# Second head pair's key squares ahead of the first columns, an early one-column exponential, and V's ones and a weight split behind two exponentials

## The chip, the cores and the metric

The kernel runs on one core of one Trainium2 chip. The metric is the device time of one execution in microseconds; the kernel before has a median of 856.37 us over three runs (855.74 to 856.46). The core's engines run apart from one another and meet only at semaphores: TensorE (PE: matmuls and transposes), VectorE (DVE), ScalarE (ACT), GpSimd (POOL) and the DMA queues, most of whose transfers SyncE (SP) issues. Each engine takes its instructions strictly in the order in which the program lists them, so an instruction that waits also holds everything queued behind it on its engine.

## The reference

One layer of a streaming encoder, for 512 prompt tokens and 32 sample tokens, all in float32, shortened:

```python
xn = rms_norm(x, g_mix_norm)
c_q, c_kv, k_r, u, gate_a, gate_b = split(xn @ w_in)
q = rms_norm(c_q, g_q_a) @ w_q_b                 # 16 heads of 64 + 32
kv = concat(past_lat, rms_norm(c_kv)) @ w_kv_b   # keys 64, values 64 per head
s = rms_norm(q_nope) . rms_norm(k_nope) + rope(q_rope) . rope(k_r)
attn = softmax(mask(s * scale)) @ v              # chunk-causal, 16 heads
u_c = causal_dwconv(u, width 4)                  # 1024 channels
r, i = sigmoid(u_c @ w_rg), sigmoid(u_c @ w_ig)
a = exp(-8 r softplus(-lam)); h_t = a h_(t-1) + sqrt(1 - a^2) i u_c
x = x + (sigmoid(gate_a) attn + sigmoid(gate_b) h) @ w_out
up = causal_dwconv(rms_norm(x, g_ffn_norm) @ w_up, width 3)
x = x + (silu(gate) * val) @ w_down
```

The layer is computed for the prompt (no past) and for the sample (512 cached positions).

## The kernel before

**Numbers as two halves.** Every large product is made in three passes. A weight tile of 128 columns (an "item", 128x1024) comes by DMA into `w_raw`; ScalarE rounds it into `w_hi` (`split_hi`), VectorE subtracts to get the rest, `w_lo` (`split_lo`), and TensorE multiplies hi·hi, hi·lo and lo·hi. Items 4 to 15 are the columns of `w_in` that stand ahead of attention; items 16 onward (`I_IN + 12` is item 16) are gate columns, multiplied inside the attention. SyncE issues the load of item t only when `w_lo` of item t-4 is done.

**Stages.** Up to 80 us the latents and the first columns are made. Then eight channel blocks of the gated recurrence run beside the first products: each block needs a convolution, two sigmoids, a tanh, an exponential, a square, a square root and a scan along time on VectorE (`recurrence(n)`, which raises the semaphore `recurrence_done`). At about 146 us the attention starts: eight steps `attend(p)`, each for one pair of heads, until about 405 us. After it come the output product and the feed-forward block, in which TensorE multiplies almost without a break.

**The order is written out by hand.** Each engine has its own block with its own `attend(p)`, and its place in the list decides when something is done; nothing is reordered by a scheduler. A step p has nine score tiles, n = 0 to 8. For a tile TensorE multiplies queries and keys (`scores`), VectorE takes the row maximum (`row_max`), ScalarE the exponential (`exps`), TensorE transposes the probabilities (`transpose_probs`), ScalarE copies them to SBUF (`probs_columns`), and TensorE multiplies them with V (`values`). `scores(p, n)` for n from 2 on waits for the exponential of tile n-2.

**The preparation of the pairs is laced into it.** For pair q ScalarE copies key and query products out of PSUM (`evacuate_kq`), squares the keys (`squares_keys`, into the buffer `kqs`) and then the queries (`squares_queries`, into the same buffer, so after VectorE's `key_sums`); VectorE sums the squares (`key_sums`, `query_sums`), takes inverse roots by ten small chained steps (`inverse_roots`) and scales keys and queries; GpSimd rotates the queries. While `attend(0)` runs for pair 0, pair 1 is normalised and pair 2 is projected. In VectorE's `attend(0)` the order is row maximum of tile 2, query sums of pair 1, inverse roots, row maximum of tile 3.

**Two guards at the entry.** The first `probs_columns` waits for more than its transpose, because its target shares memory with a recurrence buffer:

```python
act.wait_ge(s_pt, p * 9 + (n + 1))
...
if p == 0 and n == 0:
    act.wait_ge(s_rec, 6)
```

`s_rec` is `recurrence_done`, and the sixth scan is `recurrence(5)`. And `values(0, 0)` waits for `value_ones(0)`, three ScalarE copies that write the ones beside V from which the softmax sums come. ScalarE's functions come in tables; the exponential needs another one than the square root, and a load stands in the program (ACT_TABLE_LOAD) where it changes. Copy and Square need no load.

Of the kernel before, what the change touches and what calls it, by code (L numbers as in the profile page):

```python
# [20 lines left out]
P = 128  # L21
# [115 lines left out]
def layer(nc, i, c, o):  # L137
# [3 lines left out]
    with ctx:  # L141
# [9 lines left out]
        def fixed(name, shape, dtype=F32):  # L151
            nonlocal place
            n = int(np.prod(shape[1:])) * 4
            t = at(name, shape, place, dtype)
            place += -(-n // 32) * 32
            return t
# [13 lines left out]
        raw = fixed("w_raw", [P, 4, KD * P])  # L170
        hi = fixed("w_hi", [P, 2, KD * P], F32R)
        lo = fixed("w_lo", [P, 2, KD * P], F32R)
        region = place

        U = fixed("U", [P, KD, LEAD + TU])
# [506 lines left out]
        def _(act):  # L682
# [151 lines left out]
            def split_item(t):  # L834

                split_hi(t, t, loaded(t))
# [15 lines left out]
            def squares_keys(q):  # L852

                kn3 = Kn[q % 2][:, :, :, :].rearrange("p t h n -> p (t h n)")
                act.wait_ge(s_kqf, q * 6 + 3)
                if q == 0:
                    act.wait_ge(s_rec, 3)
                else:
                    act.wait_ge(s_kqm, q * 2)
                    act.wait_ge(s_qr, q)  # L860
                nc.scalar.activation(kqs[:, :], kn3, ACT.Square).then_inc(s_kqs, 1)
# [17 lines left out]
            def value_ones(s):  # L879

                if s == 0:
                    act.wait_ge(s_iu, KD - 1)
                    act.wait_ge(s_lru, KD)
                else:
                    act.wait_ge(s_rec, KD)
                full = NKT - 1
                nc.scalar.activation(V[:, s, 0:full, 1, :], ones[:, 0:VD].unsqueeze(1).to_broadcast([P, full, VD]), ACT.Copy)
                nc.scalar.activation(V[LASTP:, s, full, 1, :], ones[LASTP:, 0:VD], ACT.Copy)
                nc.scalar.activation(V[0:LASTP, s, full, :, :].rearrange("p h n -> p (h n)"), zero[0:LASTP, 0:1].to_broadcast([LASTP, 3 * VD]),
                                     ACT.Copy).then_inc(s_clear, 1)  # L890
# [14 lines left out]
            def probs_columns(p, n):  # L905

                act.wait_ge(s_pt, p * 9 + (n + 1))
                if p or n >= 2:
                    act.wait_ge(s_pv, p * 9 + n - 1)
                if p == 0 and n == 0:  # L910
                    act.wait_ge(s_rec, 6)
                b = (n + p) % 2
                w = width(n) if n < 8 else 2 * P + R2
                nc.scalar.activation(PT[:, b, 0:w], PS[:, 6 + b, 0:w], ACT.Copy).then_inc(s_ptf, 1)  # L914
# [21 lines left out]
            def columns_left(q, v, bank):  # L936

                par, bank = q % 2, PS[:, bank, :]
                act.wait_ge(s_tr, q * 5 + (v + 1))
                if q == 1 and v == 0:  # L940
                    act.wait_ge(s_bt, 6)
                if v < 2:
                    last = nc.scalar.activation(KT[0:NOPE, 2 * par + 1, v * 512:(v + 1) * 512], bank[NOPE:, :], ACT.Copy,
                                                scale=gkn[NOPE:, :])
                else:
                    if q == 0:
                        act.wait_ge(s_m2, KD)
                    last = nc.scalar.activation(QT[0:QK, 2 * par, 0:SEQ], bank[0:QK, :], ACT.Copy)
                last.then_inc(s_tra, 1)

            def attend(p):

                kq, following = p + 2 < NP_, p + 1 < NP_
                for n in range(9):
                    if n < 8:
                        exps(p, n + 1)
                    elif following:
                        exps(p + 1, 0)
                    probs_columns(p, n)
                    if kq and n < 3:  # L960
                        evacuate_kq(p + 2, 2 * n, 0)
                        evacuate_kq(p + 2, 2 * n + 1, 1)
                    if n == 0 and p == 0:
                        squares_queries(1)
                        act.wait_ge(s_free, 11)
                        gate_tanh(gate("A", 1))
                    if n == 1 and p == 0:
                        split_item(I_IN + 13)
                        act.wait_ge(s_free, 12)
                        gate_tanh(gate("B", 1))  # L970
                    if n == 1 and 1 <= p <= 5:
                        act.wait_ge(s_gf, 4 * p)
                        gate_tanh(gate(*gate_of(15 + 2 * p)))
                        split_item(17 + 2 * p)
                    if following and n == 3:
                        columns_left(p + 1, 0, 0)
                        columns_left(p + 1, 1, 1)
                    if following and n == 5:
                        columns_left(p + 1, 3, 1)
                    if n == 5 and p < 7:  # L980
                        split_item(18 + 2 * p if p < 5 else 23 + p)
                    if p == 7 and n == 6:
                        output_split_hi(2)
                    if n == 4 and kq:
                        squares_keys(p + 2)
                    if p == 0 and n == 6:
                        last_states()
                    if n == 7:
                        head_sums(p, 0)
                        if kq:  # L990
                            squares_queries(p + 2)
                    if n == 6:
                        if p == 0:
                            value_ones(1)
                        if following:
                            evacuate_v(p + 1, 0, 1)
                            act.wait_ge(s_gf, 2 * (fills(p)[0] - I_G) + 2)
                            gate_tanh(gate(*gate_of(fills(p)[0])))
                    if p == 6 and n >= 6:
                        mixed_hi(n - 6)  # L1000
                    if p == 7 and n < 3:
                        mixed_hi(3 + n)
                    if p == 7 and n == 8:
                        mixed_hi(6)
                if following:
                    evacuate_v(p + 1, 1, 0)
                    evacuate_v(p + 1, 2, 1)
                head_sums(p, 1)
                sample_parts(p)
# [30 lines left out]
                evacuate_kq(1, u, 4 + u)  # L1040
            for u in range(4, 6):
                evacuate_kq(1, u, u - 4)
            split_item(I_IN + 12)
            for v in (0, 1, 3):
                columns_left(0, v, 4 + v)
            for u in range(3):
                evacuate_v(0, u, (0, 1, 7)[u])
            exps(0, 0)
            value_ones(0)
            squares_keys(1)  # L1050
            for p in range(NP_):
                attend(p)
            output_split_hi(3)
# [65 lines left out]
        def _(dve):  # L1119
# [120 lines left out]
            def recurrence(n):  # L1240

                a_n = U[:, n, LEAD:]
                dve.wait_ge(s_h0, n + 1)
                nc.vector.tensor_tensor_scan(a_n, a_n, uc(n), 0.0, ALU.mult, ALU.add).then_inc(s_rec, 1)
# [33 lines left out]
            def key_sums(q):  # L1278
                dve.wait_ge(s_kqs, q * 2 + 1)
                nc.vector.tensor_reduce(small[:, 0, 0:NKH], sq3, X, ALU.add).then_inc(s_kqm, 1)  # L1280
# [40 lines left out]
            def row_max(p, n):  # L1321

                dve.wait_ge(s_s, p * 9 + (n + 1))
                bank, sm = score_bank(p, n), small[:, 4 + n % 3, :]
                if n < 8:
                    nc.vector.tensor_reduce(sm[:, 2:3], bank[:, 0:width(n)], X, ALU.max, negate=True).then_inc(s_mx, 1)
                else:
                    link(nc.vector.tensor_reduce(sm[:, 3:4], bank[:, 0:HP], X, ALU.max, negate=True))
                    nc.vector.tensor_reduce(sm[0:R2, 4:5], bank[0:R2, HP:HP + DEC], X, ALU.max, negate=True)
                    link(nc.vector.tensor_copy(sm[0:R2, 5:6], sm[R2:, 3:4]))  # L1330
                    link(tt(sm[0:R2, 2:3], sm[0:R2, 3:4], sm[0:R2, 4:5], ALU.min))
                    link(tt(sm[0:R2, 2:3], sm[0:R2, 2:3], sm[0:R2, 5:6], ALU.min))
                    nc.vector.tensor_copy(sm[R2:, 2:3], sm[0:R2, 2:3]).then_inc(s_mx, 1)

            def split_item(t):

                split_lo(t, t)
# [198 lines left out]
            columns(0, 4, 3)  # L1536
            row_max(0, 0)
            row_max(0, 1)
            recurrence(5)
            split_item(I_IN + 12)  # L1540
            key_sums(1)
            for p in range(NP_):
                attend(p)
            gated_sample(7)
# [645 lines left out]
```

## Time and profile before

| | us |
|---|---|
| median of three runs | 856.37 |
| the profiled execution, its own time | 856.38 |
| its span in the trace | 854.6 |
| PE busy | 837.5 (98%) |
| DVE busy | 569.0 (67%) |
| ACT busy | 363.2 (43%) |
| POOL busy | 201.0 (24%) |

The profile page gives each engine's busy time in the span, the chain of waits that ended last, and groups of instructions. Below it, the timeline lists single instructions of one engine: when they start and how long they take, where a start may come before the end of the one ahead (the engine overlaps them), so that the step from start to start is what an instruction costs its queue. An idle time stands in brackets, with what ended it.

### The profile page before, as it was taken

What the parts mean: (1) busy time and instruction counts of PE and PEld (TensorE: products, weight loads), DVE (VectorE), ACT (ScalarE), POOL (GpSimd) and SP (SyncE); (2) the same over time, 40 slices, a digit from 0 to 9 for tenths busy, and PEclk for the clock granted to TensorE, in tenths of its full rate; (3) what the DMA queues carried; (4) which work ended last, traced back from release to release, by engine and by line L of the source; (5) the groups of instructions that cost most, each with busy time, mean ns of one, the idle gap of its engine ahead of it and who ended that gap; (6) DMA issues with size and microseconds to landing.
All of it is one profiled execution on the core that took longest, in us unless ns stands there. A gap on an engine that the chain in (4) does not pass through costs nothing.

```text
span 854.6 us, 16810 instructions
## 1 busy us (share of the span) xinstructions
PE 837.5 (98%) x6540; PEld 801.0 (94%) x6540; DVE 569.0 (67%) x1059; ACT 363.2 (43%) x606; POOL 201.0 (24%) x229
## 2 busy tenths in 40 slices
PE   7999999999999999999999999999999999999998
PEld 6999898889998899877999999999999999999998
DVE  5695779877667676787646888888777776222121
ACT  5636859666545565566245222222212221222121
POOL 3122213202112021121140444333443344010000
PEclk9999999999999999999999999999999999999999
DMA  8533321131110200100222233232332323233321
GB/s 227 143 91 87 101 54 35 41 81 39 41 50 17 53 26 29 50 5 23 74 87 87 74 99 98 74 98 77 94 90 82 93 73 94 86 106 100 106 57 41
DMA packets 114467, 63.73 MB, mean 75 GB/s; under 512 B 7660, under 2 KB 112878, under 8 KB 114412
## 3 DMA queue, kind: packets, MB, share of 16 engines
q1 hardware_dynamic: 112428, 59.25, 24.5%
q0 software_dynamic: 1936, 3.70, 1.8%
q8 instruction: 38, 0.62, 0.3%
q14 instruction: 17, 0.14, 0.1%
q10 hardware_dynamic: 48, 0.02, 0.0%
HBM read 59.85 MB, written 2.70 MB: 73 GB/s over the span
## 4 chain that ended last, share of the span: by engine, by line
PE 86%; DVE 7%; ACT 4%; issue 2%; DMA 0%; SPq 0%; POOL 0%; ACTq 0%; POOLq 0%; DVEq 0%
PE PS L1650 47%; PE PS L1819 9%; PE PS L1902 6%; PE PS L1874 4%; PE PS L1836 4%; PE PS L1778 2%; PE PS L1856 2%; PE PS L2109 2%; PE PS L1810 2%; PE PS L1708 2%; PE PS L1774 1%; PE PS L1741 1%; PE PS L1800 1%; DVE w_lo L1129 1%; PE PS L1662 1%
## 5 line engine op out<-in xcount | busy, mean ns | idle before, releaser
L693 ACT ACTIVATE w_hi<-w_raw 128x1024 fp32r<-128x1024 f32 (+2 forms) x102 | 105.5, 1034 | 291.4 <-PE PS L1650 280.8
L1129 DVE TENSOR_TENSOR w_lo<-w_raw,w_hi 128x1024 fp32r<-128x1024 f32 (+2 forms) x102 | 126.0, 1235 | 106.2 <-ACT w_hi L693 106.1
L1650 PE MATMUL PS<-x2h,w_hi 128*128 128x272 f32 x704 | 145.7, 288 | 0.0
L1650 PE MATMUL PS<-x2h,w_lo 128*128 128x272 f32 x704 | 145.7, 288 | 0.0
L1650 PE MATMUL PS<-x2l,w_hi 128*128 128x272 f32 x704 | 145.1, 288 | 0.0
L1650 PEld LDWEIGHTS PS<-x2h,w_hi 128*128 128x128 f32 x704 | 110.8, 188 | 0.1
L1650 PEld LDWEIGHTS PS<-x2l,w_hi 128*128 128x128 f32 x704 | 110.6, 189 | 0.0
L1650 PEld LDWEIGHTS PS<-x2h,w_lo 128*128 128x128 f32 x704 | 109.9, 189 | 0.0
L654 POOL TENSOR_TENSOR uct<-uct 128x512 f32<-128x512 f32 x22 | 28.4, 1293 | 165.0 <-DVE uct L1603 165.0
L1650 PE MATMUL PS<-hh,w_hi 128*128 128x272 f32 x308 | 64.2, 289 | 0.0
L1650 PE MATMUL PS<-hh,w_lo 128*128 128x272 f32 x308 | 63.8, 289 | 0.0
L1650 PE MATMUL PS<-hl,w_hi 128*128 128x272 f32 x308 | 63.5, 288 | 0.0
L1819 PE MATMUL PS<-xnh,w_hi 128*128 128x272 f32 x192 | 57.2, 298 | 0.2 <-DVE KT L1313 0.2
L1819 PE MATMUL PS<-xnh,w_lo 128*128 128x272 f32 x192 | 55.6, 290 | 0.0
L1819 PE MATMUL PS<-xnl,w_hi 128*128 128x272 f32 x192 | 55.1, 287 | 0.0
L585 POOL TENSOR_TENSOR rot<-Qn,rope 128x320 f32<-128x320 f32 x16 | 14.5, 924 | 169.8 <-DVE Qn L1303 169.8
L914 ACT ACTIVATE PT<-PS 128x128 f32<-128x128 f32 (+4 forms) x72 | 31.3, 434 | 52.0 <-PE PS L1856 48.6
L1836 PE MATMUL PS<-KT,QT 100*128 100x128 f32 (+3 forms) x128 | 46.8, 448 | 3.6 <-ACT Pn L900 2.4
L1650 PEld LDWEIGHTS PS<-hh,w_hi 128*128 128x128 f32 x308 | 48.4, 188 | 0.1
L1650 PEld LDWEIGHTS PS<-hl,w_hi 128*128 128x128 f32 x308 | 48.4, 188 | 0.0
L1650 PEld LDWEIGHTS PS<-hh,w_lo 128*128 128x128 f32 x308 | 48.1, 189 | 0.0
L1874 PE MATMUL PS<-PT,V 128*128 128x128 f32 x320 | 47.0, 278 | 0.0
(303 smaller groups left out, 1849.2 us busy)
## 6 DMA issues: line engine op xcount, KB each, us to landing
w_raw<-in_w_up_dram SPq DMA_DIRECT2D x44, 512.0 KB, 3.8
w_raw<-in_w_in_dram SPq DMA_DIRECT2D x24, 512.0 KB, 3.9
w_raw<-in_w_down_dram SPq DMA_DIRECT2D x16, 512.0 KB, 4.1
w_raw<-in_w_out_dram SPq DMA_DIRECT2D x8, 512.0 KB, 4.1
w_raw<-in_w_down_dram SPq DMA_DIRECT2D x8, 384.0 KB, 3.9
xnat<-in_x_prompt_dram SPq DMA_DIRECT2D x4, 512.0 KB, 5.3
w_raw<-in_w_in_dram SPq DMA_DIRECT2D x4, 416.0 KB, 6.7
wq<-in_w_q_b_dram SPq DMA_DIRECT2D x8, 192.0 KB, 2.6
```

The lines of the kernel that those rows point to most:

```text
L654: nc.gpsimd.tensor_tensor(h_j[:, 0:SEQ], uct[:, j, 0:SEQ], h_j[:, 0:SEQ], ALU.mult)
L693: nc.scalar.activation(hi[:, slot % 2, 0:n], raw[:, slot % 4, 0:n], ACT.Copy).then_inc(s_hi, 1)
L914: nc.scalar.activation(PT[:, b, 0:w], PS[:, 6 + b, 0:w], ACT.Copy).then_inc(s_ptf, 1)
L1129: tt(lo[:, slot % 2, 0:n], raw[:, slot % 4, 0:n], hi[:, slot % 2, 0:n].bitcast(F32), ALU.subtract).then_inc(s_lo, 1)
L1650: last = mm(joined_half(2 * rank, j), w[:, slot % 2, cols], x[:, k0 + k, j * HT:(j + 1) * HT], start=(k0 + k == 0 and first), stop=(k0 + k ...
L1708: last = mm(PS[:, 3 + t, 0:LAT], x[:, k, w0:w0 + P], w[:, t4 % 2, cols], start=(k == 0 and w is hi and x is xnh), stop=(k == KD - 1 and w ...
L1778: last = mm(bank[:, a * 2 * QK:(a + 1) * 2 * QK], cqT[:, k, c0 - p0:c0 - p0 + P], wq[:, q % 2, k, :], start=(k == 0), stop=(k == NQ - 1))
L1810: last = mm(PS[:, bank, a * P:(a + 1) * P], latT[:, k0:k0 + P], wkv[:, q % 2, 1, :], start=True, stop=True)
L1819: last = mm(PS[:, j, 0:HT], w[:, item % 2, cols], x[:, k, j * HT:(j + 1) * HT], start=(k == 0 and first), stop=(k == KD - 1 and w is lo))
L1836: mm(bank[:, 0:w], QT[0:QK + NT, 2 * par + h, t * P:(t + 1) * P], KT[0:QK + NT, 2 * par + h, 0:w], start=True, stop=True).then_inc(s_s, 1)
L1874: last = mm(values_bank(h)[:, t * P:(t + 1) * P], V[:, par, a, h:h + 2, :].rearrange("p h n -> p (h n)"), PT[:, b, a * P:(a + 1) * P], sta ...
L1902: last = mm(PS[:, 2 * (r % 4) + j, 0:HT], w[:, cols], x[:, k, j * HT:(j + 1) * HT], start=(k == 0 and first), stop=(k == KD - 1 and w is w ...
```

## The change

Four edits in the order, and one new tile of one column:

1. On ScalarE `squares_keys(1)`, the key squares of pair 1, move ahead of the first `columns_left`, to where the split of item 16 stood.
2. A new exponential of one column (`exp_row`, from zeros), of which nothing is read, stands between the columns and V's copies. The table load for the exponential thereby stands there too.
3. `value_ones(0)` and the split of item 16 move into `attend(0)`, behind the exponentials of tiles 0 and 1 and behind the first `probs_columns`.
4. On VectorE `key_sums(1)` moves ahead of `recurrence(5)`.

```diff
+        row = fixed("exp_row", [P, 1])
...
                     probs_columns(p, n)
+                    if n == 0 and p == 0:
+                        value_ones(0)
+                        split_item(I_IN + 12)
...
-            split_item(I_IN + 12)
+            squares_keys(1)
             for v in (0, 1, 3):
                 columns_left(0, v, 4 + v)
+            nc.scalar.activation(row[:, :], zero[:, 0:1], ACT.Exp)
             for u in range(3):
                 evacuate_v(0, u, (0, 1, 7)[u])
             exps(0, 0)
-            value_ones(0)
-            squares_keys(1)
...
             row_max(0, 1)
+            key_sums(1)
             recurrence(5)
             split_item(I_IN + 12)
-            key_sums(1)
```

On ScalarE, from the end of pair 1's copies to the first exponential, this stood before (w_hi is the split, KT and QT are the first columns, Pn the exponential):

```order
L693 ACTIVATE w_hi<-w_raw 128x1024 [waits w_item_multiplied,w0_in]
L943 ACTIVATE KT<-PS,gkn 64x512 [waits kq_transposed] x2
L948 ACTIVATE QT<-PS 96x512 [waits lru_m2,kq_transposed]
L877 ACTIVATE V<-PS 128x4x2x64 [waits v_product] x2
L877 ACTIVATE V<-PS 32x2x64 [waits v_product]
L900 ACT_TABLE_LOAD
L900 ACTIVATE Pn<-PS,small 128x128 [waits score_max]
```

and this stands in the same place now:

```order
L862 ACTIVATE kqs<-Kn_76 128x1152 [waits q_rotated,kq_mean,kq_evacuated]
L944 ACTIVATE KT<-PS,gkn 64x512 [waits kq_transposed] x2
L949 ACTIVATE QT<-PS 96x512 [waits lru_m2,kq_transposed]
L1050 ACT_TABLE_LOAD
L1050 ACTIVATE exp_row<-zero 128x1
L878 ACTIVATE V<-PS 128x4x2x64 [waits v_product] x2
L878 ACTIVATE V<-PS 32x2x64 [waits v_product]
L901 ACTIVATE Pn<-PS,small 128x128 [waits score_max]
```

The key squares have taken the split's place, and the table load stands three copies earlier.

On ScalarE, from behind that first exponential to the query squares of pair 1 (kqs from Qn), before:

```order
L887 ACTIVATE V<-ones 128x8x64 [waits lru_gates,lru_gated_input]
L888 ACTIVATE V<-ones 32x64
L889 ACTIVATE V<-zero 96x192
L861 ACTIVATE kqs<-Kn_75 128x1152 [waits q_rotated,kq_mean,kq_evacuated]
L900 ACTIVATE Pn<-PS,small 128x256 [waits score_max]
L914 ACTIVATE PT<-PS 128x128 [waits recurrence_done,probs_transposed]
L846 ACTIVATE Kn_73<-PS 128x512 [waits kq_transposed,kq_product]
L846 ACTIVATE Kn_73<-PS 128x512 [waits kq_product]
L868 ACTIVATE kqs<-Qn_76 128x960 [waits kq_mean,kq_evacuated]
```

and now:

```order
L901 ACTIVATE Pn<-PS,small 128x256 [waits score_max]
L915 ACTIVATE PT<-PS 128x128 [waits recurrence_done,probs_transposed]
L888 ACTIVATE V<-ones 128x8x64 [waits lru_gates,lru_gated_input]
L889 ACTIVATE V<-ones 32x64
L890 ACTIVATE V<-zero 96x192
L694 ACTIVATE w_hi<-w_raw 128x1024 [waits w_item_multiplied,w0_in]
L847 ACTIVATE Kn_74<-PS 128x512 [waits kq_transposed,kq_product]
L847 ACTIVATE Kn_74<-PS 128x512 [waits kq_product]
L869 ACTIVATE kqs<-Qn_77 128x960 [waits kq_mean,kq_evacuated]
```

The copy of the probabilities (PT), which waits for the scan, has moved from behind the ones and the key squares to ahead of the ones and the split.

On VectorE, around the sixth scan (U from U, uc), before:

```order
L1326 TENSOR_REDUCE small<-PS 128x1 [waits scores] x2
L1244 SCALAR_TENSOR_TENSOR U<-U,uc_90 128x548 [waits sample_state_set]
L1129 TENSOR_TENSOR w_lo<-w_raw,w_hi 128x1024 [waits w_hi_done]
L1280 TENSOR_REDUCE small<-kqs 128x18 [waits kq_squares]
L1326 TENSOR_REDUCE small<-PS 128x1 [waits scores]
L1284 TENSOR_REDUCE small<-kqs 128x10 [waits kq_squares]
```

and now:

```order
L1329 TENSOR_REDUCE small<-PS 128x1 [waits scores] x2
L1283 TENSOR_REDUCE small<-kqs 128x18 [waits kq_squares]
L1247 SCALAR_TENSOR_TENSOR U<-U,uc_91 128x548 [waits sample_state_set]
L1132 TENSOR_TENSOR w_lo<-w_raw,w_hi 128x1024 [waits w_hi_done]
L1329 TENSOR_REDUCE small<-PS 128x1 [waits scores]
L1287 TENSOR_REDUCE small<-kqs 128x10 [waits kq_squares]
```

The key sums have gone ahead of the scan; TensorE's, GpSimd's and SyncE's lists are as before.

## Rows read from the trace of the kernel before

**Rows 1.** The page: the chain that ended last, by engine.
```profile
PE 86%; DVE 7%; ACT 4%; issue 2%; DMA 0%; SPq 0%; POOL 0%; ACTq 0%; POOLq 0%; DVEq 0%
```

**Rows 2.** Windows of the attention's entry and its rest: length, busy time per engine, clock.
```profile
147.00:160.00 13.00, 10.54 (x68) 8.72 (x67) 11.13 (x25) 11.67 (x24) 0.00 (x0) 1.00 0.27 65
...
176.00:405.00 229.00, 226.18 (x1813) 200.82 (x1812) 165.79 (x361) 133.91 (x272) 38.85 (x38) 1.00 0.13 35
```

**Rows 3.** Timeline of PE at the entry: start, duration, instruction, idle before.
```profile
148.63 0.91 PE L1836 MATMUL PS<-KT,QT 100*128 100x384 f32 x2 [1.34 <-ACT Pn L900]
149.38 0.27 PE L1856 MATMUL PS<-ident,Pn 128*128 128x128 f32 x1
...
154.34 0.49 PE L1836 MATMUL PS<-KT,QT 100*128 100x128 f32 x2
...
158.63 0.70 PE L1836 MATMUL PS<-KT,QT 100*128 100x256 f32 x2 [1.08 <-ACT Pn L900]
...
161.50 0.39 PE L1819 MATMUL PS<-xnh,w_hi 128*128 128x272 f32 x1 [0.19 <-DVE KT L1313]
```

**Rows 4.** Timeline of ACT at the entry.
```profile
142.05 1.09 ACT L693 ACTIVATE w_hi<-w_raw 128x1024 fp32r<-128x1024 f32 x1
143.17 1.26 ACT L943 ACTIVATE KT<-PS,gkn 64x512 f32<-64x512 f32 x2
144.45 0.59 ACT L948 ACTIVATE QT<-PS 96x512 f32<-96x512 f32 x1
145.11 0.60 ACT L877 ACTIVATE V<-PS 128x512 f32<-128x512 f32 x1
146.00 0.89 ACT L877 ACTIVATE V<-PS 128x512 f32<-128x512 f32 x2 [0.29 <-PE PS L1810]
146.91 1.28 ACT L900 ACT_TABLE_LOAD   x1
148.21 0.37 ACT L900 ACTIVATE Pn<-PS,small 128x128 f32<-128x128 f32 x1
148.47 0.62 ACT L887 ACTIVATE V<-ones 128x512 f32<-128x512 f32 x1
...
149.64 1.15 ACT L861 ACTIVATE kqs<-Kn 128x1152 f32<-128x1152 f32 x1
150.69 0.45 ACT L900 ACTIVATE Pn<-PS,small 128x256 f32<-128x256 f32 x1
151.05 0.26 ACT L914 ACTIVATE PT<-PS 128x128 f32<-128x128 f32 x1
151.20 1.07 ACT L846 ACTIVATE Kn<-PS 128x512 f32<-128x512 f32 x2
152.26 1.01 ACT L868 ACTIVATE kqs<-Qn 128x960 f32<-128x960 f32 x1
...
157.89 0.69 ACT L900 ACTIVATE Pn<-PS,small 128x512 f32<-128x512 f32 x1 [1.29 <-DVE small L1326]
...
174.06 0.23 ACT L818 ACTIVATE st<-U 128x16 f32<-128x16 f32 x1
```

**Rows 5.** Timeline of DVE at the entry.
```profile
146.89 0.86 DVE L1326 TENSOR_REDUCE small<-PS 128x1 f32<-128x128 f32 x2 [0.78 <-PE PS L1836]
147.78 1.30 DVE L1244 TENSOR_TENSOR_SCAN U<-U,uc 128x548 f32<-128x548 f32 x1
149.00 1.20 DVE L1129 TENSOR_TENSOR w_lo<-w_raw,w_hi 128x1024 fp32r<-128x1024 f32 x1
150.82 1.35 DVE L1280 TENSOR_REDUCE small<-kqs 128x18 f32<-128x1152 f32 x1 [0.62 <-ACT kqs L861]
152.09 0.55 DVE L1326 TENSOR_REDUCE small<-PS 128x1 f32<-128x384 f32 x1
153.30 0.82 DVE L1284 TENSOR_REDUCE small<-kqs 128x10 f32<-128x640 f32 x1 [0.67 <-ACT kqs L868]
...
157.16 0.69 DVE L1326 TENSOR_REDUCE small<-PS 128x1 f32<-128x512 f32 x1
```

## The prediction

> **What bounds the kernel now.** I read the page first: the chain that ended last lies for 86% on PE [rows 1], so the time changes only by what PE loses or gains in gaps. Then the windows: from 147 to 160 us PE is busy 10.54 of 13.00 us, and from 176 to 405 us 226.18 of 229 [rows 2]. The change touches only this entry into the attention. Then PE's timeline, for the gaps: three of them, 1.34 us before 148.63, 1.08 us before 158.63 and 0.19 us before 161.50, together 2.61 us [rows 3]. That is all there is to win here. Last ACT's and DVE's timelines, for who ends them.
>
> The first gap ends with tile 0's exponential, 148.21 to 148.58 [rows 3, 4]. Ahead of it on ACT stand V's copies, held up 0.29 us by PE, and the table load of 1.28 us [rows 4].
>
> The second gap looks as if the exponential of tile 3 were its cause (157.89). But that one waited 1.29 us for its row maximum, DVE's 157.16, and DVE did nothing but work from 153.30 to there: query sums and inverse roots of pair 1 stand ahead of that maximum. They started when ACT's query squares ended, 152.26 + 1.01 = 153.27 [rows 4, 5]. And up to 153.27 ACT had run without a pause from 146.00 [rows 4]. So the quantity to follow is **the start of the query squares on ACT, 152.26**. Exponential, maximum and PE's tile 5 follow it by fixed distances: 157.16 - 152.26 = 4.90, 158.63 - 152.26 = 6.37.
>
> **The change part by part.** What stands ahead of the query squares is not fewer instructions than before: key squares and split have changed places, and the one column is new. Only the order can help, so I run the queues through.
>
> *Key squares for the split, at 142.05.* The split cost 1.12 us of the queue, up to the start of the columns at 143.17. The key squares cost 1.05 (149.64 to 150.69) and last 1.15 against 1.09 [rows 4]. Their own waits are long met. I take 0 to +0.1 us for the columns, 0.08 in the middle.
>
> *Table load and one column.* They start when QT is done, 144.45 + 0.59 + 0.08 = 145.12. The load takes 1.28 + 0.02, to 146.42 [rows 4]. A one-column exponential is not in the trace; the nearest row is the copy of 16 columns, 0.23 us [rows 4]. Bounds are 0.1 and 0.37 (the 128-column exponential); I take 0.2, since it is nearest to the former. V's copies start at 146.62, now without a wait for PE, whose products let the second start at 146.00. Three copies cost 0.5 + 0.5 + 0.27 (0.60 for one, 0.89 for two, with 0.1 of overlap) [rows 4]. Tile 0's exponential so starts at 147.87 instead of 148.21, and ends at 148.24. Its row maximum is there by 147.4 (the two end at 147.75) [rows 5]. PE's tile 2 starts at 148.28, a gap of 0.99 instead of 1.34: **-0.35 us**, on PE, at this place.
>
> *Tile 1's exponential.* It follows at 148.15 and ends by 148.6. It was at 150.69. That it is 2.5 us earlier brings nothing by itself: PE's tile 3, which waits for it, stands behind tile 2 (0.91), a transpose and pair 2's key products, and would begin at 151.28 - 0.35 either way.
>
> *The copy of the probabilities, PT.* Now it comes next on ACT, and it has two waits. The transpose starts 0.75 us behind PE's tile 2 (149.38 - 148.63) and takes 0.27 [rows 3], so it is done at 149.30. The other is the sixth scan. Before, DVE had it from 147.78 to 149.08, and PT, at 151.05, never saw it. Now the key sums stand ahead of it: they start at 147.77, since ACT has had the squares since 143.2, and cost 152.09 - 150.82 = 1.27 [rows 5]. The scan runs from 149.04 to 150.34. **PT can't start before 150.36**, and ACT stands idle for some 1.75 us from 148.6. Queued behind PT on ACT are the ones, the split, pair 2's two key copies and the query squares.
>
> *From PT to the query squares.* PT 0.15 (151.05 to 151.20), the ones 1.17 (148.47 to 149.64), the split 0.99 to 1.12 (1.09 less the overlap of 0.10, or its step of before), two key copies 1.06 (151.20 to 152.26) [rows 4]. With 1.0 for the split: 150.36 + 0.15 + 1.17 + 1.0 + 1.06 = 153.74, against 152.26. **+1.48 us.** The low end, with the lowest of each, is +1.4; the high end, with 1.12 for the split and 0.1 for handing over the semaphore, +1.7.
>
> *DVE behind it.* It is idle from 150.34 until the split's w_hi is there at 152.75, then w_lo costs 1.2 and tile 2's maximum 0.5 [rows 5], to 154.45. The query sums want to start at 153.74 + 1.03 = 154.77, so DVE is in time by 0.3 us. Roots and tile 3's maximum then start at 158.64, its exponential at 159.37 and PE's tile 5 at 160.11, each 1.48 later. Pair 1's scaling and columns on DVE follow the same chain, so the gap before 161.50 stays and nothing is caught up.
>
> *PE in between.* Its values of tile 0 want the ones (now 151.7, before 149.73) and come at about 152. Pair 2's third key product wants the copy that starts at 152.68 and ends at 153.25, so a gap of about 0.9 us opens. Tile 4 wants tile 2's exponential, which stands behind the query squares on ACT and comes 1.48 later: PE at 155.82 instead of 154.34 [rows 3]. The early 0.35 us is spent waiting, and the gaps before 155.82 grow by 1.48 + 0.35 = 1.83.
>
> *The queue of loads.* w_lo of item 16 is done near 153.95 instead of 150.20 [rows 5], so SyncE issues the load of item 20, and behind it pair 1's key-mask and rope transfers into the second half of KT, some 3.7 us later. Item 20 and those tables are wanted from 174 us on, when `attend(1)` begins, so I cost this at nothing; without that cover it would be at most the 3.7.
>
> **Sum.** -0.35 at the first gap, then +1.83 in the gaps up to tile 4, which is +1.48 at tile 4 and at tile 5, and 0 afterwards: 226.18 busy of 229 us leaves PE little idle time, and what there is there waits on chains that have moved with it [rows 2]. The profiled execution took 856.38 us, its span 854.6; it is 0.01 above the median of 856.37, so no correction. 856.38 + 1.48 = **857.9 us**, a loss of 0.17%. What a measurement here can tell from no change is about 0.2%, 1.7 us, so by that yardstick this is "the same", close to its edge.
>
> **The rivals.**
> *A, the scan is no hindrance.* If PT could go with its transpose, at 149.33, ACT's query squares would start at 152.71, +0.45: 856.8 us. For it: only that DVE may reach the scan a little sooner. Against: 1.27 us of key sums stand ahead of it, and PT's second wait. That the change shortens anything is already excluded here, as PT's transpose alone comes too late.
> *B, the loss is caught up.* After 176 us PE is idle 2.82 us in all [rows 2]. If some of it hung on an absolute time (a transfer), part of the 1.48 would vanish: 856.3 to 857.2. Against: the DMA share is 0.13 in that stretch, and the gaps at the entry end with ACT and DVE.
> *C, faster.* If tile 5 hung on exponentials and not on the query squares, the early exponentials would close both big gaps: up to -2.42, 854.0 us. Against: the 1.29 us wait of ACT for the row maximum.
> *D, slower, DVE becomes the bound.* In VectorE's list w_lo and tile 2's maximum now stand between the late split and the query sums. Their margin is 0.3 us; each 0.1 that w_hi, w_lo or the maximum takes beyond that comes on top. It decides for slower by over 0.2% from 0.55 us more than I give them. With 1.0 more: 858.6 us.
> *E, slower, the clock.* PE would stand still in four gaps of 0.6 to 1.1 us within 13 us. Before, with gaps of 1.34 and 1.08 in the same stretch, the granted clock stayed at 1.00, 2.4 GHz [rows 2]. At 1.2 GHz the 10.5 us of PE work there would take up to twice as long, of which half a stretch would already cost 5: 863 us. The Trainium skill (TensorE: Matmul & The Clock Gate, Part 1) says that the gate halves the clock after idling and gives it back after sustained work, which speaks against a change that spreads more idle time over this stretch; by that rule this case would be the forecast, by the row's 1.00 it is remote.
>
> **Chances.** The forecast 0.74; its own range is 857.3 to 858.5, and 0.25 of the 0.74 lies above 858.08, where "slower" begins, because a few tenths in the handing over or in the split are enough. A 0.08, B 0.07, C 0.04, D 0.04, E 0.03. Faster by over 0.2%: C and a little of B, 0.05. Slower: 0.25 + 0.04 + 0.03 = 0.32. The same: 0.63. The range is 856.6 to 858.9: it takes in A, the upper part of B and D, and leaves out C and E and the lower part of B, with a tenth for what lies beyond.
>
> **What would show it.** In the profile of the changed kernel: tile 0's exponential near 147.9; ACT idle by some 1.7 us before PT, ended by DVE's scan; the scan from about 149.0; ACT's query squares near 153.7; DVE idle before w_lo, ended by w_hi; PE's gap before tile 2 near 1.0, new gaps before pair 2's third key product and before tile 4, and tile 5 near 160.1. From there on every stage should stand 1.5 us later. I am wrong if PT starts at its transpose (A), if the query squares start before 153, if PE's shift at 161.5 is not the shift at the end (B), if DVE and not ACT ends last before the query sums (D), or if the clock in the stretch is under 1.00 (E).

## The result: 0.26% slower, and the profile after

| | us |
|---|---|
| kernel before, median of 21 runs | 855.86 (855.28 to 856.78) |
| changed kernel, median of 21 runs | 857.86 (857.30 to 859.23) |
| ratio | 1.0026, 95% interval 1.0020 to 1.0032 |
| the profiled execution of the changed kernel, its own time | 858.23 |
| its span | 856.4 |

The change costs 2.0 us by the medians. (Their quotient is 1.0023. The ratio in the table and those below are a reckoning of their own over the single runs, and differ from the quotient of the medians by up to 0.0005.) The forecast of 857.9 is met, but partly by luck: it stood on a profiled execution of 856.38, while the kernel before has a median of 855.86 over more runs. The forecast loss was 1.48 us, the measured one 2.0, so a term of 0.5 us was missing. The starting point stood 0.5 too high and the loss 0.5 too low, and the two cancelled. Below the missing 0.5 turns out to be real and to lie nowhere near the entry.

The entry itself went as worked out. This is the timeline of ScalarE in the changed kernel (start, duration, instruction, idle time before it and its releaser), to be read against [rows 4]:

```profile
145.05 1.28 ACT L1050 ACT_TABLE_LOAD   x1
146.34 0.20 ACT L1050 ACTIVATE exp_row<-zero 128x1 f32<-128x1 f32 x1
146.45 1.36 ACT L878 ACTIVATE V<-PS 128x512 f32<-128x512 f32 x3
147.84 0.73 ACT L901 ACTIVATE Pn<-PS,small 128x128 f32<-128x128 f32 x2
150.31 0.28 ACT L915 ACTIVATE PT<-PS 128x128 f32<-128x128 f32 x1 [1.74 <-DVE U L1247]
150.49 0.62 ACT L888 ACTIVATE V<-ones 128x512 f32<-128x512 f32 x1
...
151.65 1.04 ACT L694 ACTIVATE w_hi<-w_raw 128x1024 fp32r<-128x1024 f32 x1
152.60 1.06 ACT L847 ACTIVATE Kn<-PS 128x512 f32<-128x512 f32 x2
153.55 1.00 ACT L869 ACTIVATE kqs<-Qn 128x960 f32<-128x960 f32 x1
...
159.18 0.69 ACT L901 ACTIVATE Pn<-PS,small 128x512 f32<-128x512 f32 x1 [1.31 <-DVE small L1329]
```

Both exponentials are done by 148.6, then ScalarE stands for 1.74 us until VectorE's scan ends, where before it had no gap from 146.00 to the query squares. The query squares start at 153.55 instead of 152.26. VectorE, against [rows 5]:

```profile
146.77 0.86 DVE L1329 TENSOR_REDUCE small<-PS 128x1 f32<-128x128 f32 x2 [0.78 <-PE PS L1839]
147.66 1.35 DVE L1283 TENSOR_REDUCE small<-kqs 128x18 f32<-128x1152 f32 x1
148.93 1.29 DVE L1247 TENSOR_TENSOR_SCAN U<-U,uc 128x548 f32<-128x548 f32 x1
152.72 1.23 DVE L1132 TENSOR_TENSOR w_lo<-w_raw,w_hi 128x1024 fp32r<-128x1024 f32 x1 [2.51 <-ACT w_hi L694]
...
154.58 0.82 DVE L1287 TENSOR_REDUCE small<-kqs 128x10 f32<-128x640 f32 x1 [0.16 <-ACT kqs L869]
```

The scan starts behind the key sums at 148.93 instead of 147.78, and holds up ScalarE; then VectorE waits 2.51 us for ScalarE's split. TensorE, against [rows 3]:

```profile
148.26 0.91 PE L1839 MATMUL PS<-KT,QT 100*128 100x384 f32 x2 [1.09 <-ACT Pn L901]
...
153.23 0.49 PE L1777 MATMUL PS<-wkv,latT 128*128 128x128 f32 x2 [0.85 <-ACT Kn L847]
...
155.62 0.49 PE L1839 MATMUL PS<-KT,QT 100*128 100x128 f32 x2 [0.34 <-ACT Pn L901]
...
159.92 0.70 PE L1839 MATMUL PS<-KT,QT 100*128 100x256 f32 x2 [1.08 <-ACT Pn L901]
...
162.78 0.39 PE L1822 MATMUL PS<-xnh,w_hi 128*128 128x272 f32 x1 [0.18 <-DVE KT L1316]
```

Tile 2's gap has shrunk by 0.25 us (1.34 to 1.09), two new ones stand at 153.23 and before tile 4 (155.62), and tile 5 comes 1.29 us later (159.92 instead of 158.63). This execution ran 0.12 us early at its first row maximum (146.77 against 146.89), so the loss by tile 5 is 1.41 us. The gap of 1.08 before tile 5 is unchanged, as is the one on DVE's KT.

### The profile page after: what moved, and what is told of

The parts are those of the page before. It is cut to its first block, busy times and chain, and to the rows that moved or that the text cites. A ratio compares the mean times of both kernels' runs of the same rounds, so it can differ in the third digit from the quotient of the medians.

```text
span 856.4 us, 16811 instructions
## 1 busy us (share of the span) xinstructions
PE 838.6 (98%) x6540; PEld 801.3 (94%) x6540; DVE 572.3 (67%) x1059; ACT 363.0 (42%) x607; POOL 200.8 (23%) x229
## 4 chain that ended last, share of the span: by engine, by line
PE 86%; DVE 7%; ACT 4%; issue 2%; DMA 0%; SPq 0%; POOL 0%; ACTq 0%; POOLq 0%; DVEq 0%
PE PS L1653 47%; PE PS L1822 9%; PE PS L1905 6%; PE PS L1839 4%; PE PS L1877 4%; PE PS L1781 2%; PE PS L1859 2%; PE PS L2112 2%; PE PS L1813 2%; PE PS L1711 2%; PE PS L1777 1%; PE PS L1744 1%; PE PS L1803 1%; DVE w_lo L1132 1%; PE PS L1665 1%
```

## The experiments

All runs of a group shared their runs of the kernel before, whose median was 855.99, 855.97 and 856.02 us in the three groups. The bounds given are 95% intervals of the ratio. Beside the times I cut every profile into the same stages, from the first and last starts of certain TensorE instructions. "Entry" runs from the last product of the gated recurrence (124.0 us before) to the first product of the sample's fold in `attend(1)` (186.9 before); "attention" from there to the last such product (405.1 before); "tail" from that to the end of the span. Within the tail, "out" runs to the first product of `x2h`, "up" runs from the first product of `x2h` to the first of `hh`, and "down" from there to the end.

| kernel | median, against before | entry | attention | tail | out | up | down |
|---|---|---|---|---|---|---|---|
| before | | 62.9 | 218.2 | 449.5 | 43.2 | 265.6 | 140.7 |
| changed | +2.00 | 64.3 | 218.2 | 450.0 | 42.8 | 266.2 | 141.0 |
| e1, scan first | +1.39 | 63.3 | 218.3 | 450.0 | 42.8 | 266.2 | 141.0 |
| e2, one column only | +0.21 | 62.6 | 218.2 | 450.0 | 42.8 | 266.2 | 141.0 |
| e3, no move behind | +0.13 | 62.4 | 218.3 | 450.1 | 42.8 | 266.3 | 141.0 |
| e5, queries first | -1.37 | 60.8 | 218.2 | 450.1 | 42.9 | 266.2 | 141.0 |
| e6, tile only, 32 bytes | +0.62 | 62.9 | 218.3 | 450.0 | 42.8 | 266.2 | 141.0 |
| e7, changed, no tile | +1.50 | 64.3 | 218.2 | 449.4 | 43.2 | 265.6 | 140.6 |
| e8, queries first, no tile | -1.93 | 60.8 | 218.2 | 449.5 | 43.2 | 265.7 | 140.6 |
| e9, tile of 64 bytes | -1.17 | 62.8 | 218.1 | 448.7 | 43.0 | 265.1 | 140.6 |
| e10, queries first, 64 bytes | -0.89 | 60.7 | 218.1 | 448.7 | 43.0 | 265.1 | 140.6 |
| e11, tile of 128 bytes | -0.49 | 62.8 | 218.3 | 449.0 | 42.8 | 265.7 | 140.5 |

The stages before the entry are missing from the table: they ended between 123.1 and 124.4 us in these profiles, in no visible relation to what was changed, which is why stages are compared here and not spans alone. What entry, attention and tail lost or gained adds up to the difference of the medians within 0.4 us for every kernel but one, e10.

**e1: the scan first again.** The changed kernel, with this undone on VectorE:

```diff
-            key_sums(1)
             recurrence(5)
+            key_sums(1)
             split_item(I_IN + 12)
```

> The changed kernel with one thing undone: on VectorE the sixth scan stands ahead of pair 1's key sums again. Theory (the copy of the probabilities waits for the scan, and that wait is the loss): the scan ends 1.27 us earlier, the copy starts with its transpose near 149.3 instead of 150.3, ScalarE's wait before it shrinks from 1.74 to about 0.7 us, query squares start near 152.6, PE's tile 5 near 158.95; against the kernel before +0.45 us, so 856.3 where before has 855.9, and 1.0 us less than the changed kernel at the entry. Rival (the wait is harmless, the loss comes from the ones and the split standing behind the exponentials, or from somewhere behind the entry): tile 5 stays at 159.9 and the time at +1.4 to +2.0.

Measured: 857.38 us, ratio 1.0016 (1.0007 to 1.0025). This execution stood 0.6 us early at its first row maximum (146.29 against 146.89). ScalarE's timeline:

```profile
148.85 0.28 ACT L915 ACTIVATE PT<-PS 128x128 f32<-128x128 f32 x1 [0.75 <-PE PS L1859]
...
152.09 0.99 ACT L869 ACTIVATE kqs<-Qn 128x960 f32<-128x960 f32 x1
```

The wait has shrunk from 1.74 to 0.75 us, and it is now TensorE's transpose that ends it, which is the bound that the prediction gave for this copy. The entry takes 63.3 us, 1.0 less than in the changed kernel and 0.4 more than before: the theory, to a tenth. But the time is +1.39 and not +0.45, which by itself would be the rival's +1.4. The tail is 0.5 us longer, as in the changed kernel; the stages make +1.0 of the +1.39, and the rest is within the interval (+0.6 to +2.1 us).

**e2: the one-column exponential alone.** The kernel before, with the tile and this line:

```diff
                 columns_left(0, v, 4 + v)
+            nc.scalar.activation(row[:, :], zero[:, 0:1], ACT.Exp)
```

> The kernel before with edit 2 alone: the one-column exponential ahead of V's copies. Theory (ScalarE runs without a pause from V's copies to the query squares, so what it saves at their head arrives at tile 5): tile 0's exponential 0.35 us earlier, query squares at 151.9, tile 5 at 158.3, time -0.35 us. Rival (the early start is eaten by a wait further on, as it was in the changed kernel): query squares stay at 152.2 and the time at 0.

Measured: 856.20 us, ratio 1.0001 (0.9992 to 1.0010). By the time alone the rival has won. ScalarE and TensorE say otherwise:

```profile
147.89 0.37 ACT L901 ACTIVATE Pn<-PS,small 128x128 f32<-128x128 f32 x1
...
151.94 1.00 ACT L869 ACTIVATE kqs<-Qn 128x960 f32<-128x960 f32 x1
```

```profile
148.31 0.91 PE L1838 MATMUL PS<-KT,QT 100*128 100x384 f32 x2 [0.98 <-ACT Pn L901]
...
158.31 0.70 PE L1838 MATMUL PS<-KT,QT 100*128 100x256 f32 x2 [1.08 <-ACT Pn L901]
```

Query squares and tile 5 come 0.32 us earlier, as expected, and the entry is 0.3 us shorter. Again the tail is 0.5 us longer, and takes that gain away.

**e3: ones and split not moved.** The changed kernel without edit 3:

```diff
             exps(0, 0)
+            value_ones(0)
+            split_item(I_IN + 12)
             for p in range(NP_):
                 attend(p)
...
                     probs_columns(p, n)
-                    if n == 0 and p == 0:
-                        value_ones(0)
-                        split_item(I_IN + 12)
```

> The changed kernel without edit 3: V's ones and the split of item 16 stand between tile 0's and tile 1's exponentials, as the ones did before; key squares early, one-column exponential and key sums ahead of the scan stay. Theory: the scan still ends at 150.3, but the copy of the probabilities comes to ScalarE's head only at about 150.65, behind ones and split, so it waits for nothing; query squares near 151.85, tile 5 near 158.2, -0.4 us against the kernel before and -1.9 against the changed one at the entry. Rival (the scan's later end costs by itself, whatever stands before the copy): +1 us and more against before.

Measured: 856.12 us, ratio 1.0001 (0.9992 to 1.0010). ScalarE:

```profile
150.12 0.45 ACT L901 ACTIVATE Pn<-PS,small 128x256 f32<-128x256 f32 x1
150.47 0.26 ACT L915 ACTIVATE PT<-PS 128x128 f32<-128x128 f32 x1
...
151.59 1.01 ACT L869 ACTIVATE kqs<-Qn 128x960 f32<-128x960 f32 x1
```

The scan is as late as in the changed kernel, and the copy does not wait for it. The entry takes 62.4 us, 1.9 less than in the changed kernel and 0.5 less than before. The time is +0.13 all the same and not the -0.4 expected, as the tail is 0.6 longer. So with edits 1 and 2 in place a late scan alone costs nothing (e3, -0.5 against before). Ones and split behind the copy bring the entry from there to +0.4 with an early scan (e1), and to +1.4 with a late one: by the difference of these entries the move costs 0.9 us, an estimate that takes the late scan to cost nothing without it, and the late scan another 1.0 on top. The version with neither, edits 1 and 2 alone, was not run.

**e5: query squares first.** Built on the theory that pair 1's query squares set the pace of this stretch; several things move at once, so its gain belongs to the whole order and not to one edit. V's ones go to GpSimd, idle there, and the splits out of the way:

```diff
             exps(0, 0)
-            value_ones(0)
-            squares_keys(1)
+            squares_queries(1)
...
                     if n == 0 and p == 0:
-                        squares_queries(1)
+                        split_item(I_IN + 12)
...
+            key_sums(1)
             row_max(0, 0)
             row_max(0, 1)
             recurrence(5)
-            split_item(I_IN + 12)
-            key_sums(1)
...
+            pool.wait_ge(s_iu, KD - 1)
+            pool.wait_ge(s_lru, KD)
+            step.on(nc.gpsimd.memset(V[:, 0, 0:NKT - 1, 1, :], 1.0))
+            pool.wait_ge(s_pool, step.value())
+            step.on(nc.gpsimd.memset(V[LASTP:, 0, NKT - 1, 1, :], 1.0))
```

(shown against the kernel before; key squares and the one column stand as in the changed kernel, a third memset writes V's zeros, and VectorE's w_lo of item 16 stands behind the scaling of pair 1.)

> A version after the theory that pair 1's query squares set the pace: V's ones are written by GpSimd (three memsets after the starts of blocks 3 to 5), the query squares stand on ScalarE directly behind tile 0's exponential, the split of item 16 behind the copies of pair 2's first keys, on VectorE the key sums stand ahead of the first two row maxima and w_lo of item 16 behind pair 1's scaling. Theory: query squares near 148.2, DVE's query sums start near 150, tile 3's maximum waits for PE and not for the roots, PE's gap before tile 5 (1.08) goes and the one before tile 2 shrinks by 0.2 to 0.35; -1.3 to -1.6 us against the kernel before, 854.4. Rival (tile 5 hangs on exponentials or products, not on the query squares): the gap before tile 5 stays and the time is within 0.4 us of before.

Measured: 854.62 us, ratio 0.9985 (0.9976 to 0.9994). TensorE's timeline, in which tile 5 has no idle time ahead of it any more:

```profile
148.29 0.91 PE L1845 MATMUL PS<-KT,QT 100*128 100x384 f32 x2 [1.09 <-ACT Pn L908]
...
153.77 0.47 PE L1845 MATMUL PS<-KT,QT 100*128 100x128 f32 x2
...
156.80 0.60 PE L1845 MATMUL PS<-KT,QT 100*128 100x256 f32 x2
```

and ScalarE's:

```profile
148.13 0.99 ACT L876 ACTIVATE kqs<-Qn 128x960 f32<-128x960 f32 x1
149.03 0.46 ACT L908 ACTIVATE Pn<-PS,small 128x256 f32<-128x256 f32 x1
149.38 0.28 ACT L922 ACTIVATE PT<-PS 128x128 f32<-128x128 f32 x1
150.24 0.60 ACT L854 ACTIVATE Kn<-PS 128x512 f32<-128x512 f32 x1 [0.58 <-PE PS L1783]
```

With the query squares at 148.13 the copies of pair 2's keys wait for TensorE and not the other way round. The entry is 2.1 us shorter, more than the 1.3 to 1.6 expected; the tail takes back 0.6, and the time of -1.37 is inside the expected bounds.

**e6 to e8: where the half microsecond in the tail is.** Every kernel so far had the new one-column tile. It takes 32 bytes of each partition ahead of the shared region, so all of attention's and the feed-forward block's buffers stand 32 bytes higher (the recurrence's too, but not the weight buffers `w_raw`, `w_hi` and `w_lo`, which lie ahead of it). e6 is the kernel before with nothing but this line, e7 and e8 are the changed kernel and e5 without it:

```diff
+        row = fixed("exp_row", [P, 1])
```

```diff
-        row = fixed("exp_row", [P, 1])
...
-            nc.scalar.activation(row[:, :], zero[:, 0:1], ACT.Exp)
+            nc.scalar.activation(zero[:, 3:4], zero[:, 0:1], ACT.Exp)
```

> The kernel before with the one-column tile alone: it is allocated and never written, no instruction is added or moved, but every buffer laid out behind it (the shared region: attention's and the feed-forward block's buffers) stands 32 bytes higher. All kernels with this tile so far lost 0.5 to 0.7 us between the end of attention and the end of the program, where PE has no gap. Theory (the loss there is the place of the buffers in memory): +0.5 us, all of it behind 405 us, with DVE busy longer in the up-projection. Rival (it comes from the added exponential or from what precedes): 0.

> The changed kernel, whose one-column exponential writes to the unused last column of the zeros tile, so that there is no new tile and all buffers stand where they stood before; every instruction is there. Theory of the memory place: the loss at the entry stays (+1.4 at tile 5) and the 0.5 behind 405 us goes: +1.4 to +1.5 against the kernel before, 857.4. Rival (the added instruction or the shift in time does it): +2.0, 857.9.

> The version with pair 1's query squares first and V's ones on GpSimd (-1.37 us measured, -2.1 at the end of attention), with its one-column exponential written to the unused column of the zeros tile. Theory of the memory place: -1.9 to -2.1 us against the kernel before, 853.9. Rival: -1.4 as it was.

Measured: e6 856.59 us, ratio 1.0009 (1.0000 to 1.0018); e7 857.47, 1.0021 (1.0012 to 1.0030); e8 854.04, 0.9978 (0.9969 to 0.9987). By the medians an unused tile costs 0.6 us, the change without it 1.50, for a forecast of 1.48, and e8 gains 1.93. The medians alone don't prove the 0.6, since the interval of e6 begins at no change, and that 1.50 comes so near to 1.48 is partly chance, with an interval of some 1.0 to 2.6 us. The tails do: 449.4 to 449.5 us in the three profiles without the tile (before, e7, e8), 450.0 to 450.1 in the six with it at 32 bytes. The views of single TensorE lines, e6 first, then e7 (shortest, median and longest duration in ns, then first and last start in us):

```profile
L1651 PE MATMUL PS<-x2l,w_hi x704: 285/287/293, 448.7 to 714.2; 128*128 128x272 f32 x176
L1651 PE MATMUL PS<-hh,w_hi x308: 283/288/372, 714.6 to 833.0; 128*128 128x272 f32 x154
```

```profile
L1652 PE MATMUL PS<-x2l,w_hi x704: 283/288/291, 449.0 to 714.0; 128*128 128x272 f32 x176
L1652 PE MATMUL PS<-hh,w_hi x308: 286/288/373, 714.4 to 832.5; 128*128 128x272 f32 x154
```

The same products, in the same order and with no gap, take 265.5 us from first to last start in e6 and 265.0 in e7. TensorE isn't waiting there; its matmuls follow one another a little faster or slower, by where the buffers lie. The windows from 460 to 700 us say the same, in before, e6 and e9 (a step of 64 bytes, below): TensorE busy for all of the 240 us, at the same granted clock of 1.00, with 1918, 1914 and 1922 matmuls.

```profile
460.00:700.00 240.00, 240.00 (x1918) 240.00 (x1917) 195.07 (x326) 58.72 (x63) 89.29 (x80) 1.00 0.30 87
```

```profile
460.00:700.00 240.00, 240.00 (x1914) 240.00 (x1913) 196.95 (x326) 58.68 (x64) 88.35 (x80) 1.00 0.30 87
```

```profile
460.00:700.00 240.00, 240.00 (x1922) 240.00 (x1922) 194.70 (x328) 58.14 (x61) 89.25 (x80) 1.00 0.30 87
```

All six profiles with the tile at 32 bytes have 1914, the three without it 1918 or 1919, the two at 64 bytes 1922 and 1923, and the one at 128 bytes (e11) 1918.

**e9 to e11: other steps.** e9 is the kernel before with an unused tile of 16 columns, 64 bytes; e11 the same with 32 columns, 128 bytes; e10 is e5 with its tile at 16 columns.

```diff
+        row = fixed("exp_row", [P, 16])
```

> The kernel before with an unused tile of 16 columns, so that every buffer behind it stands 64 bytes higher instead of 32. Theory (it is the 32-byte step that matters, which takes the buffers off multiples of 64): 0 against the kernel before. Rival (any shift of the layout costs): +0.5.

> The kernel before with an unused tile of 32 columns, so that the buffers behind it stand 128 bytes higher. If multiples of 64 bytes are all alike, this gives what the 64-byte shift gave, -1.2 us; if the place in a coarser pattern counts, anything between -1.2 and +0.6, and 0 would say that 128 bytes is the period.

> The version with the query squares first, its one-column tile widened to 16 columns, so that the buffers behind it stand 64 bytes higher than in the kernel before. Theory (the entry's gain of 2.0 and the 1.2 that the 64-byte shift gave by itself add up, since one lies before 162 us and the other mostly outside the entry): -3.1 us against the kernel before, 852.9. Rival (the 1.2 us was a chance of those runs, or hangs on the old order): -2.0, 854.0.

Measured: e9 854.80 us, ratio 0.9984 (0.9974 to 0.9994); e11 855.53, 0.9992 (0.9983 to 1.0002), not told from no change; e10 855.13, 0.9985 (0.9976 to 0.9994). I had e9 wrong: 64 bytes are not neutral, they gain. Its tail is 0.8 us shorter than before, and e11's 0.5 shorter. I had e10 wrong too: -0.89 us, against -3.1 expected and -2.0 for the rival. The execution that was profiled has e8's entry and e9's tail, and took 853.46 us, 2.9 less than the one profiled before. But the eleven runs lie between 851.80 and 855.47 us, seven of them above 855, while those of e8 lie between 853.34 and 855.02. So the two gains add up in the profile and not in the median, and with e8's order the step of 64 bytes made the median 1.0 us worse, where with the old order it made it 1.2 better; the intervals of e8 and e10 overlap, so this much is open as well. What the other runs of e10 spent is open, since no profile shows them.

The fastest version measured is e8, 854.04 us, with the ratio of 0.9978 to the kernel before given above; it beats the changed kernel too, which was at 857.86 us beside nearly the same time of before (855.86, against 855.97).

## Why the prediction was right, and where it was short

- **What sets the pace of the entry.** Right. The query squares of pair 1, not the exponentials, decide when tile 5 comes. They moved by 0.32 in e2, 1.29 in the changed kernel, and tile 5 moved by the same 0.32 and 1.29. e5, built on that reading, closed the gap before tile 5. The fixed distances held as well: in the changed kernel tile 3's maximum stands 4.90 us behind the query squares (158.45) and tile 5 6.37 us, both as before. In e5 they no longer hold: the query squares come 4.13 us earlier and tile 5 only 1.83, since TensorE has no gap left there and sets the pace itself.
- **The wait for the scan.** Right, in kind and size: forecast 1.75 us of ScalarE idle until the scan, measured 1.74. e1 takes 1.0 us of it away by putting the scan first, e3 all of it by keeping other work in front of the copy.
- **The early table load.** Tile 0's exponential at 147.87 forecast, 147.84 measured, but in an execution that stood 0.12 us early, and by two misses that cancel: the one column cost its queue 0.11 us and not 0.2 (146.34 to 146.45), V's copies 1.39 and not 1.27. The gap before tile 2 is 1.09 instead of the forecast 0.99; in e2, which leaves the split in its old place, it is 0.98, so the 0.1 is what the key squares cost more than the split ahead of the columns. As forecast it was worth nothing in the changed kernel, while it is worth 0.3 us in e2, where nothing behind it waits.
- **From the copy to the query squares.** 3.24 us (150.31 to 153.55) for a forecast of 3.38. The two key copies cost 0.95 instead of 1.06, the split 0.95 instead of 1.0, below the lowest of my bounds (0.99), and the copy itself 0.18 instead of 0.15. Against that the copy started 0.07 later than forecast, once the 0.12 is allowed for. That is why the entry lost 1.4 and not 1.48.
- **The queue of loads.** SyncE issues the load of item 20 at 153.98 instead of 150.23, 3.75 us later for a forecast of 3.7, and it cost nothing, as forecast: the first product of the fold in `attend(1)` comes 1.3 us later, like tile 5.
- **VectorE as the next bound (rival D).** It stood ready only 0.16 us ahead of the query squares, for a forecast of 0.3. It did not decide, but was closer than I gave it.
- **"0 afterwards" in the sum.** This is the step that failed. I asked what there was to wait for behind the entry, and found nothing; that is right, as attention takes 218.2 us in both. But I did not price the new tile. I called it one column that is never read, and it moved every buffer behind it by 32 bytes: +0.6 us by itself (e6, 0.5 of it in the tail), mostly in a stretch where TensorE has no gap at all. With it the loss is 2.0 and not 1.5 us.
- **The chances.** "The same" was given 0.63 and "slower" 0.32, with the border at 0.2%. The ratio is 1.0026, slower, its interval from the border upwards. The entry alone, 1.4 us or 0.16%, would have been on the side I favoured, and the missing term carried it over; e7, which measures the change without that term, can't confirm this, since its ratio of 1.0021 (1.0012 to 1.0030) lies on the border.
- **The rivals.** A is excluded by the 1.74 us wait, B by the equal length of attention and a tail that did not get shorter, C by the 1.31 us for which tile 3's exponential still waits for its maximum. E is excluded by the clock: the row for 147 to 160 us of the changed kernel reads 1.00 with PE busy 9.63 of 13.00 us.

```profile
147.00:160.00 13.00, 9.63 (x58) 7.66 (x57) 9.74 (x22) 9.88 (x22) 0.00 (x0) 1.00 0.26 64
```

The Trainium skill's rule on the clock gate (TensorE: Matmul & The Clock Gate, Part 1), that idling halves the clock, did not come into play here: 3.37 us without work, in several pieces, left it at 2.4 GHz.

## What to carry to other kernels

Before moving work behind an instruction, look up every semaphore that this instruction waits for, also those that never cost anything: a guard that was covered by the work in front of it becomes a wait once that work is gone, and everything moved behind it pays. When several instructions of a chain can be the pacemaker, follow the wait of the last one back to the engine that had no gap; an instruction that starts 2.5 us earlier (tile 1's exponential) is worth nothing if the chain doesn't run through it. And a new buffer is not free because nobody reads it: put it into an unused corner, as e7 and e8 do, or measure it alone, as e6 does, and compare a change's stages with the kernel before, stage by stage, before believing a total.

## What I had not expected of the hardware

In the feed-forward block, where TensorE is busy all the time in every profile (240.00 of 240.00 us between 460 and 700, the granted clock 1.00), the place of the buffers in memory changes the time. Against the kernel before (449.5; 449.4 and 449.5 in e7 and e8, whose buffers lie as before) the tail from the end of attention took +0.5 us with the buffers 32 bytes higher (six profiles, all between 450.0 and 450.1 us), -0.8 us at 64 bytes (two, both 448.7) and -0.5 us at 128 bytes (one, 449.0). The sign differs by stage: 32 bytes take 0.3 to 0.4 us off "out" and add 0.6 to "up" and 0.3 to "down". In the up-projection VectorE's small copies of the carried rows look like a cause at first: in e6 they take 346 ns on average and in e9 291.

```profile
L1594 DVE COPY upx<-vec 128x2 f32 (+1 forms) x41 | 14.2, 346 | 0.0
```

```profile
L1594 DVE COPY upx<-vec 128x2 f32 (+1 forms) x41 | 11.9, 291 | 0.0
```

(The first is of e6, the second of e9, both in the window from 460 to 700 us.) But they do not go with the tail: they take 309 ns in the kernel before and 293 in e8, whose tails are equal, and 346 to 398 ns among the six profiles at 32 bytes, whose tails are equal too. Whether TensorE's reads collide with those of the other engines or the alignment of its own reads is at work, these runs don't tell.
